# Feed-forwards in two parts of 14 and 8 gated tiles, with more chunks by seven block products

## The chip, the cores and the metric

The kernel runs on one core of a Trainium2 chip. The metric is the device time of one launch in microseconds. Data are fp32; the kernel splits each operand of a large product into a high and a low part and forms the product by three matmuls.

## The reference

Two blocks run one after the other over a sequence of 512 tokens of width 1024. The first has two layers of feed-forward, mixer, feed-forward and per-layer embedding (PLE); the second has two layers of mixer and feed-forward, scaled and shifted by a vector that a "modulation" product `silu(c) @ w_ada` gives. What the change touches is the six feed-forwards:

```python
def swiglu(h, w1, w3, w2):
    return (jax.nn.silu(h @ w1) * (h @ w3)) @ w2
def half_ffn(x, g, w1, w3, w2):                       # four times
    return x + FFN_RES * swiglu(rmsnorm(x, g), w1, w3, w2)
# second block, twice:
x = x + g2 * swiglu_2(h, w_gate_up[l], w_down[l])
```

with `h` of 512 x 1024, `w1` and `w3` of 1024 x 2816 and `w2` of 2816 x 1024. A PLE stage, `x + sigmoid(rmsnorm(x) @ ple_gate) * (p @ ple_proj)`, follows the second and the fourth feed-forward.

## The kernel before

Activations are held transposed: a tile is 128 features by 512 tokens. The 2816 gated features are 22 tiles. Weights come by DMA in chunks of 1024 x 256 (1 MB) into three buffers `raw`; ACT copies each 128 columns (a "run") to `wh` (high), DVE subtracts to get `wl` (low), and PE then does 8 k-tiles x 3 matmuls of 512 columns. There are three pairs `wh`/`wl` of 1024 elements, so DVE can split about two runs ahead of PE. A half-size buffer holds one part of a block product.

The four programs (PE, ACT, DVE and POOL, with SP issuing the weight DMAs) each walk the same list, which `rounds` yields for a feed-forward: for chunk pairs j = 0 to 10 the w1 chunk gives gate tiles 2j and 2j+1, the w3 chunk value tiles 2j and 2j+1. There is no scheduler; each engine works in order of this list, and DVE's and ACT's `step(g)` splits whatever weights have a free buffer when PE is about to do run g. After a plain w3 run `run_done` does, on DVE and ACT in turn: product with the gate (`gv`, tile `T`), ACT's high copy (`uh`), DVE's low part (`ul`). In the first four feed-forwards ("ffn") h is not yet divided by its root mean square; the tile `R` carries that factor and DVE multiplies every w1 and every w3 tile by it.

`WOVEN` names the chunks done by seven block products in place of eight (Strassen's scheme in Winograd's form, over halves of the 1024 features and of the 512 tokens). Before, these are both chunks of j = 2 to 6 in the last two feed-forwards ("ffn2"): 10 of 22, and none in the ffns. Such a chunk is 7 parts of 4 x 3 matmuls of 256 columns, 84 in all instead of 48 of 512 columns. `PARTS` = 1, 4, 6, 5 come first, then 7; parts 3 and 2 (`rest`) are put behind the next chunk's beginning. Part 6 goes on top of part 1 in the same bank, so PE first waits for ACT to copy part 1 out (`sq<-ps`, signal `curved p1`). DVE mixes quarters of the raw weights in place (`raw<-raw`, four per chunk), splits seven halves, and puts the tiles together (`joined`). The sums and differences of h that the parts need are made once per feed-forward by `differences`, beside the runs.

The output product walks four pairs of output tiles; for each pair three chunks of w2 with 8, 8 and 6 k-tiles, both tiles in each. DVE then adds the bank to x in one instruction.

The 48 modulation chunks ("ada") are not PE work: DVE reads each raw chunk with eight 256-wide multiply-adds, turns the sum in 32 x 32 squares and reduces it. Twelve are placed in each of the four ffns (`plan_ada`).

`inputs` (POOL) fetches `p` and `ple_proj` for a PLE stage into a region that the feed-forward uses for its tiles, so it waits until PE has finished a named run of w2 (L3629). PE's `enter` waits for both to land before it begins the PLE stage.

Of the kernel before, what the change touches and what calls it, by code (L numbers as in the profile page):

```python
# [169 lines left out]
WOVEN = {s: {(w, j) for j in range(2, 7) for w in ("w1", "w3")} if s[0] == "ffn2" else set() for s in FFNS}  # L170
PARTS = (1, 4, 6, 5)
SHARE = {1: (0, 0), 5: (0, 0), 3: (0, 0), 2: (1, 0), 4: (1, 1), 6: (1, 1), 7: (0, 1)}
# [4 lines left out]

def rounds(s):

    left = None  # L180
    for j in range(11):
        for w in ("w1", "w3"):
            if (w, j) in WOVEN[s]:
                for p in PARTS:
                    yield "part", w, j, p
            else:
                yield "run", w, 2 * j, 0
            if left:
                yield "part", *left, 3
                yield "part", *left, 2  # L190
                yield "joined", *left, 0
                left = None
            if (w, j) in WOVEN[s]:
                yield "part", w, j, 7
                yield "joined", w, j, 1
                left = w, j
            else:
                yield "post", w, 2 * j, 0
                yield "run", w, 2 * j + 1, 0
                yield "post", w, 2 * j + 1, 0  # L200


def build(nc, I, out):
    with ExitStack() as ctx:
# [123 lines left out]
        def plan_ffn(key, w1, w3, w2, with_ada):  # L328
            at = {}
            for what, w, i, p in rounds(key):  # L330
                j = i if what in ("part", "joined") else i // 2
                if what in ("part", "run") and (w, j) not in at:
                    at[w, j] = len(chunks)
                    chunks.append((8, 256, [(0, (w1 if w == "w1" else w3)[:, 256 * j:256 * j + 256])]))
                n = at[w, j] if (w, j) in at else None
                if what == "part":
                    G_of[(key, w, j, "part", p)] = n_mm[0]
                    part_of[n_mm[0]] = key, w, j, p
                    order.append(("mm", n_mm[0], n, p, 0, 0, 0))
                elif what == "run":  # L340
                    G_of[(key, w, i)] = n_mm[0]
                    order.append(("mm", n_mm[0], n, 128 * (i % 2), 128, 0, 8))
                else:
                    if what == "post" and w == "w3" and i % 2 and with_ada and j > 6:
                        plan_ada(1)
                    continue
                tail[n] = (lo_split, n_mm[0])
                n_mm[0] += 1
            for m in range(4):
                for k0, kt in ((0, 8), (8, 8), (16, 6)):  # L350
                    wide(key, ("w2", k0), w2, m * 256, 256, 2 * m, k0 * 128, kt)
                    if with_ada and (m < 2 or m == 2 and k0 < 16):
                        plan_ada(1)
# [160 lines left out]
        full = ar[:, 28:36, :]  # L514
        diff = ar[:, 6:14, :].rearrange("p a n -> p (a n)").rearrange(quads, c=4, k=4)
        diff_h = uh[:, 14:22, :].rearrange("p a n -> p (a n)").rearrange(quads, c=4, k=4)
        diff_l = ul[:, 14:22, :].rearrange("p a n -> p (a n)").rearrange(quads, c=4, k=4)
# [61 lines left out]
        def pe_program(e):  # L579
# [22 lines left out]
            def freed(s, name):  # L602
# [3 lines left out]
                if s[0] == "ffn2" and name[0] == "w3":  # L606
                    return (worked, (s, "gv", name[1]))
# [243 lines left out]

            def ffn(s, nxt):
                for what, w, i, p in rounds(s):
# [4 lines left out]
                if nxt is None:  # L858
                    chain = pe.beside(output())
                for m in range(4):  # L860
# [2947 lines left out]
```

## Time and profile before

| | us |
|---|---|
| time, median of 3 runs (range) | 3154.97 (3154.47 to 3155.27) |
| profiled execution's own time | 3154.14 |
| its span, first to last instruction | 3152.2 |
| PE busy | 3132.3 |
| DVE busy | 2013.7 |
| ACT busy | 1236.3 |

The profiled execution is 0.8 us below the median of the runs; 1.9 us of its time lie outside the span. PE's busy time counts a matmul from its start to its modelled end, so 99% says that PE hardly ever waits, not how dense its work is; the distance between two starts shows that.

### The profile page before, as it was taken

The numbers are of one execution on the slowest core, as the hardware profiler recorded it, in microseconds if no ns is written. First come the engines' busy times: TensorE is split into PE (matmuls) and PEld (weight loads), VectorE is DVE, ScalarE is ACT, GpSimd is POOL, SyncE is SP. The second block draws the span as 40 slices with busy tenths as digits, with TensorE's granted clock in tenths as the row PEclk, the third lists the DMA queues.
The fourth block names the chain that finished last, engine by engine and source line by source line (L and its number), as shares of the span: only waits on it lengthen the run. The fifth ranks groups of instructions, "written<-read, shape, count | busy, mean of one in ns | idle before, by whom it ended". The sixth has DMA issues, their size and how long they took to land.

```text
span 3152.2 us, 38120 instructions
## 1 busy us (share of the span) xinstructions
PE 3132.3 (99%) x15408; PEld 2618.7 (83%) x15408; DVE 2013.7 (64%) x2925; ACT 1236.3 (39%) x1812; POOL 157.8 (5%) x170
## 2 busy tenths in 40 slices
PE   9999999999999999999999999999999999999999
PEld 7888878888888888888888888887898888779887
DVE  5567567446856467557644685988893368889532
ACT  5322264322233222264332223565453235745321
POOL 2000000000000000000000000122000002300000
PEclk9999999999999999999999999999999999999999
DMA  5345322334542345432232463221233332022322
GB/s 151 97 131 190 124 84 94 94 96 145 190 137 81 94 133 181 140 94 81 86 102 94 147 192 117 82 70 41 78 111 104 100 87 84 28 80 95 120 87 74
DMA packets 334341, 339.92 MB, mean 108 GB/s; under 512 B 12502, under 2 KB 329208, under 8 KB 334168
## 3 DMA queue, kind: packets, MB, share of 16 engines
q1 hardware_dynamic: 332144, 333.80, 33.4%
q0 software_dynamic: 1792, 3.62, 0.4%
q8 instruction: 124, 2.03, 0.3%
q14 instruction: 49, 0.40, 0.0%
q10 hardware_dynamic: 232, 0.06, 0.0%
HBM read 335.36 MB, written 2.10 MB: 107 GB/s over the span
## 4 chain that ended last, share of the span: by engine, by line
PE 91%; DVE 5%; ACT 3%; issue 1%; DMA 0%; SPq 0%; DVEq 0%; ACTq 0%
PE ps L138 89%; PE ps L141 2%; ACT ar L95 1%; DVE wl L100 1%; DVE ar L100 1%; DVE ar L108 1%; ACT wh L95 1%; DVE ul L100 0%; ACT L95 0%; DVE T L108 0%; DVE hl L108 0%; ACT T L95 0%; ACT sp L95 0%; DMA ar<-in_x 0%; DVE T L100 0%
## 5 line engine op out<-in xcount | busy, mean ns | idle before, releaser
L138 PE MATMUL ps<-hh,wl 128*128 128x512 f32 (+1 forms) x2680 | 1026.4, 383 | 4.6 <-DVE wl L100 4.5
L100 DVE TENSOR_TENSOR wl<-raw,wh 128x1024 fp32r<-128x1024 f32 (+3 forms) x649 | 700.6, 1081 | 500.6 <-ACT wh L95 499.0
L138 PE MATMUL ps<-hh,wh 128*128 128x512 f32 (+1 forms) x2680 | 1019.2, 380 | 0.0
L138 PE MATMUL ps<-hl,wh 128*128 128x512 f32 (+1 forms) x2680 | 1019.0, 380 | 0.0
L95 ACT ACTIVATE wh<-raw 128x1024 fp32r<-128x1024 f32 (+3 forms) x649 | 602.5, 936 | 507.7 <-PE ps L138 462.0
L138 PEld LDWEIGHTS ps<-hh,wl 128*128 128x128 f32 x2680 | 504.8, 188 | 105.7 <-issue 11.0
L138 PEld LDWEIGHTS ps<-hh,wh 128*128 128x128 f32 x2680 | 505.0, 188 | 96.6
L138 PEld LDWEIGHTS ps<-hl,wh 128*128 128x128 f32 x2680 | 505.2, 189 | 93.2 <-issue 0.2
L138 PE MATMUL ps<-ul,wh 128*128 128x512 f32 (+1 forms) x1472 | 531.6, 366 | 0.0
L138 PE MATMUL ps<-uh,wl 128*128 128x512 f32 (+1 forms) x1376 | 503.7, 366 | 6.2 <-DVE wl L100 5.1
L138 PE MATMUL ps<-uh,wh 128*128 128x512 f32 (+1 forms) x1376 | 502.2, 365 | 0.0
L138 PEld LDWEIGHTS ps<-ul,wh 128*128 128x128 f32 x1472 | 278.5, 189 | 44.6
L138 PEld LDWEIGHTS ps<-uh,wl 128*128 128x128 f32 x1376 | 260.4, 189 | 47.6 <-ACT wh L95 6.7
L138 PEld LDWEIGHTS ps<-uh,wh 128*128 128x128 f32 x1376 | 260.3, 189 | 41.3
L95 ACT ACTIVATE uh<-T 128x512 fp32r<-128x512 f32 x132 | 83.4, 632 | 444.5 <-DVE T L100 444.1
L100 DVE TENSOR_TENSOR T<-ps,R 128x512 f32<-128x512 f32 x196 | 134.0, 689 | 176.3 <-PE ps L138 153.3
L95 ACT ACTIVATE T<-T 128x512 f32<-128x512 f32 (+1 forms) x112 | 68.6, 617 | 309.4 <-DVE T L100 309.1
L108 DVE SCALAR_TENSOR_TENSOR ada<-raw,small,ada 128x256 f32<-128x256 f32 x336 | 162.9, 485 | 12.0
L100 DVE TENSOR_TENSOR ul<-T,uh 128x512 fp32r<-128x512 f32 x132 | 91.4, 693 | 81.1 <-ACT uh L95 79.6
L100 POOL TENSOR_TENSOR small<-small 128x4 f32<-128x4 f32 (+1 forms) x23 | 38.1, 1655 | 1763.2 <-DVE small L123 996.6
L95 ACT ACTIVATE ar<-ar 128x512 f32<-128x512 f32 (+6 forms) x69 | 73.2, 1075 | 93.8 <-DVE ar L100 58.2
L95 ACT ACTIVATE hh<-x,VT 128x512 fp32r<-128x512 f32 x64 | 45.2, 720 | 161.3 <-DVE x L108 123.9
(257 smaller groups left out, 2791.3 us busy)
## 6 DMA issues: line engine op xcount, KB each, us to landing
raw<-in_ffn_w SPq DMA_DIRECT2D x119, 1024.0 KB, 5.3
raw<-in_w_ada SPq DMA_DIRECT2D x48, 1024.0 KB, 5.2
raw<-in_w_gate_up SPq DMA_DIRECT2D x44, 1024.0 KB, 5.1
raw<-in_m_w_in SPq DMA_DIRECT2D x26, 1024.0 KB, 5.4
raw<-in_w_down SPq DMA_DIRECT2D x16, 1024.0 KB, 5.1
raw<-in_ffn_w SPq DMA_DIRECT2D x16, 768.0 KB, 4.3
raw<-in_w_in SPq DMA_DIRECT2D x12, 1024.0 KB, 5.3
raw<-in_m_w_out SPq DMA_DIRECT2D x8, 1024.0 KB, 5.2
```

Source lines behind the costliest of these rows:

```text
L95: return self.issue(lambda e: e.activation(out, in_, func, **kw))
L100: return self.issue(lambda e: e.tensor_tensor(out, a, b, op))
L108: return self.issue(lambda e: e.scalar_tensor_tensor(out=out, in0=a, scalar=s, in1=b, op0=op0, op1=op1))
L138: return self.issue(lambda e: e.matmul(out, l, r, start=start, stop=stop, skip_group_check=True))
L141: return self.issue(lambda e: e.transpose(out, in_, ident))
```

## The change

`WOVEN` is a new set. In the ffns it holds the w3 chunk of j = 2, all w1 chunks of j = 3 to 10 and the w3 chunks of j = 4, 6 and 8: 12 of 22. In both ffn2s it holds w3 of j = 2, w1 of 3 to 10 and w3 of 3 to 9: the table comes to 16 of 22.

`rounds` now yields the output product too, and does a feed-forward in two parts: chunks j = 0 to 6 (14 gated tiles), then w2 chunks of 8 and 6 k-tiles for all eight output tiles; then j = 7 to 10 (8 tiles) and one w2 chunk of 8 k-tiles for each pair. Each output tile is therefore added to x twice (`added`). The second part's tiles reuse the slots of the first (`u_high`, `u_low`).

In the ffns `R` no longer multiplies the w3 tiles but the output banks, ahead of the addition to x, so an addition is two DVE instructions, twice per tile. A w3 tile's bank is read directly by the product with the gate. The plain chunk that follows a w1 chunk by block products has its two posts both behind its second run.

`differences` sums h in four pieces instead of two, and starts one step later except in the first stage. A modulation chunk is summed in two interleaved chains and one final addition. The modulation chunks of an ffn are now behind w3 runs 15 and 19, eight in the first output product and two in the second. The POOL wait in `inputs` names run ("w2", 14, 7), where it named ("w2", 0, 7).

```diff
-WOVEN = {s: {(w, j) for j in range(2, 7) for w in ("w1", "w3")} if s[0] == "ffn2" else set() for s in FFNS}
+WOVEN = {s: {("w3", 2), *((w, j) for j in range(3, 11) for w in ("w1", "w3") if w == "w1" or s[0] == "ffn2" or j % 2 == 0)} - {("w3", 10)} for s in FFNS}
...
+def parts_of(s):
+    if WOVEN[s]:
+        return (range(0, 7), ((0, 8), (8, 6))), (range(7, 11), ((14, 8),))
+    return (range(0, 11), ((0, 8), (8, 8), (16, 6))),
...
+    for js, ks in parts_of(s):
+        for j in js:
+            for w in ("w1", "w3"):
+                if (w, j) in WOVEN[s]:
+                    for p in PARTS:
+                        yield "part", w, j, p
+                    if left:
+                        yield from rest()
+                    yield "part", w, j, 7
+                    yield "joined", w, j, 1
+                    left = w, j
+                    continue
                 yield "run", w, 2 * j, 0
+                if left:
+                    yield from rest()
+                    left = None
+                    yield "run", w, 2 * j + 1, 0
+                    yield "post", w, 2 * j, 0
+                else:
+                    yield "post", w, 2 * j, 0
+                    yield "run", w, 2 * j + 1, 0
                 yield "post", w, 2 * j + 1, 0
+        for m in range(4):
+            for k in ks:
+                for a in range(2):
+                    yield "out", k, 2 * m + a, (k == ks[0]) + 2 * (k == ks[-1]) + 4 * (ks[-1][0] + ks[-1][1] == FT)
+                    if left:
+                        yield from rest()
+                        left = None
...
-                        dve.ts(adab[:, 0:256], src[:, 0, :], c_act[:, 0:1], MUL).then_inc(worked, ("ada", i, 0))
-                        for t in range(1, 8):
-                            dve.own()
+                        sums = adab[:, 0:256], adab[:, 256:512]
+                        for t in range(2):
+                            dve.ts(sums[t], src[:, t, :], c_act[:, t:t + 1], MUL).then_inc(worked, ("ada", i, t))
+                        for t in range(2, 8):
+                            dve.wait_ge(worked, ("ada", i, t - 2))
...
-                if s[0] == "ffn":
-                    dve.tt(T3[a][:, :], ps((s, "w3", t))[:, :], R[:, :], MUL).then_inc(left((s, "w3", t)), (s, "w3", t))
-                    dve.own()
-                    silu_done(s, t)
-                    dve.tt(T3[a][:, :], T3[a][:, :], T1[a][:, :], MUL).then_inc(worked, (s, "gv", t))
-                else:
-                    silu_done(s, t)
-                    dve.tt(T3[a][:, :], ps((s, "w3", t))[:, :], T1[a][:, :], MUL).then_inc(worked, (s, "gv", t))
+                silu_done(s, t)
+                dve.tt(T3[a][:, :], ps((s, "w3", t))[:, :], T1[a][:, :], MUL).then_inc(worked, (s, "gv", t))
...
-                if s[0] == "ffn":
+                if s[0] == "ffn" and w == "w1":
                     dve.own()
-                    dve.tt(to, to, R[:, :], MUL).then_inc(worked, (s, "gate" if w == "w1" else "value", t))
+                    dve.tt(to, to, R[:, :], MUL).then_inc(worked, (s, "gate", t))
...
             def differences(s):
-                for h in range(2):
-                    r = slice(4 * h, 4 * h + 4)
-                    for t in range(4 * h, 4 * h + 4):
+                if s != STAGES[0]:
+                    yield 1
+                for q in range(4):
+                    r = slice(2 * q, 2 * q + 2)
+                    for t in (2 * q, 2 * q + 1):
...
+            def added(s, nxt, t, p):
+                dve.wait_ge(used, end_run(s, t, p))
+                b = ps((s, "o", p & 4, t))
+                key = (x_new, (s, t)) if p & 4 else (worked, (s, "first", t))
+                if s[0] == "ffn":
+                    dve.tt(T1[t % 2][:, :], b[:, :], R[:, :], MUL).then_inc(worked, (s, "turned", p & 4, t))
+                    x_free(s, t)
+                    dve.own()
+                    dve.stt(x[:, t, :], T1[t % 2][:, :], 0.5, x[:, t, :], MUL, ADD).then_inc(*key)
+                    return
...
-                pool.wait_ge(used, G_of[(BEFORE[s], "w2", 0, 7)])
+                pool.wait_ge(used, G_of[(BEFORE[s], "w2", 14 if WOVEN[BEFORE[s]] else 0, 7)])
```

Two places in the order of DVE. The first is in the first ffn, at chunk pairs 3 and 4. Before, a plain w3 chunk and the first run of the next pair's w1 chunk stand as follows (`wl` is the low part of a run, `T_81`, `T_82` the value tiles, `ul` their low parts):

```order
L100 TENSOR_TENSOR T_81<-ps,R 128x512 [waits lo_part,weights_used]
L100 TENSOR_TENSOR T_81<-T_81,T_78 128x512 [waits curved,emptied3]
L100 TENSOR_TENSOR ul<-T_81,uh 128x512 [waits hi_part]
L100 TENSOR_TENSOR wl_65<-raw_58,wh_62 128x1024 [waits hi_split]
L100 TENSOR_TENSOR T_82<-ps,R 128x512 [waits lo_part,weights_used]
L100 TENSOR_TENSOR T_82<-T_82,T_79 128x512 [waits curved,emptied4]
L100 TENSOR_TENSOR ul<-T_82,uh 128x512 [waits hi_part]
L100 TENSOR_TENSOR wl_66<-raw_59,wh_63 128x1024 [waits hi_split]
```

Of the changed kernel, the end of w1 of pair 3 (joined and multiplied by `R`), the two posts of w3, and the first rows of the next w1 chunk by block products:

```order
L100 TENSOR_TENSOR T_78<-ps,sq_76 128x512 [waits weights_used]
L100 TENSOR_TENSOR T_78<-T_78,R 128x512 [waits emptied2]
L100 TENSOR_TENSOR wl_66<-raw_60,wh_63 128x512 [waits hi_split]
L100 TENSOR_TENSOR T_81<-ps,T_78 128x512 [waits curved,lo_part]
L100 TENSOR_TENSOR ul<-T_81,uh 128x512 [waits hi_part]
L100 TENSOR_TENSOR T_82<-ps,T_79 128x512 [waits weights_used]
L100 TENSOR_TENSOR ul<-T_82,uh 128x512 [waits hi_part]
L100 TENSOR_TENSOR wl_64<-raw_60,wh_61 128x512 [waits hi_split]
L100 TENSOR_TENSOR raw_60<-raw_60 128x4x128 [waits lo_split]
L100 TENSOR_TENSOR wl_64<-raw_58,wh_61 128x512 [waits hi_split]
```

The two posts moved from one behind each run to both behind the second, and what follows them is the split of small parts. The second place is the ACT order at the same point of the changed kernel; `uh` are the high copies of both value tiles, `wh` the high copies of two parts, `sq_75` the copy of part 1 for which PE's part 6 waits:

```order
L95 ACTIVATE T_78<-T_78 128x512 [waits worked]
L95 ACTIVATE uh<-T_81 128x512 [waits worked]
L95 ACTIVATE uh<-T_82 128x512 [waits worked]
L95 ACTIVATE wh_61<-raw_60 128x512 [waits weights_used]
L95 ACTIVATE wh_61<-raw_58 128x512 [waits raw_in0]
L95 ACTIVATE sq_75<-ps 128x256 [waits weights_used]
```

Before, ACT has only run splits, silus and `uh` copies there:

```order
L95 ACTIVATE wh_61<-raw_58 128x1024 [waits weights_used,raw_in0]
L95 ACTIVATE uh<-T_81 128x512 [waits worked]
L95 ACTIVATE wh_62<-raw_58 128x1024 [waits weights_used]
L95 ACTIVATE uh<-T_82 128x512 [waits worked]
L95 ACTIVATE wh_63<-raw_59 128x1024 [waits weights_used,raw_in1]
```

The copy `sq_75` is new there, and it stands behind both `uh` copies.

## Rows read from the trace of the kernel before

**Rows 1.** Page: engine, busy us (share) xinstructions; chain, shares by engine.

```profile
PE 3132.3 (99%) x15408; PEld 2618.7 (83%) x15408; DVE 2013.7 (64%) x2925; ACT 1236.3 (39%) x1812; POOL 157.8 (5%) x170
...
PE 91%; DVE 5%; ACT 3%; issue 1%; DMA 0%; SPq 0%; DVEq 0%; ACTq 0%
```

**Rows 2.** Waits of PE: waiter <- releaser: total us, times, longest us.

```profile
PE ps L138 <- DVE wl L100: 9.6, 7, 3.1
...
PE ps L138 <- ACT sq L95: 1.1, 1, 1.1
```

**Rows 3.** Windows: stretch, length, busy us (x) of PE, PEld, DVE, ACT, POOL, PEclk.

```profile
600.00:760.00 160.00, 160.00 (x708) 132.53 (x707) 85.86 (x110) 47.46 (x60) 0.00 (x0) 1.00 0.36 112
2270.00:2350.00 80.00, 80.00 (x669) 80.00 (x668) 74.20 (x117) 48.28 (x95) 0.00 (x0) 1.00 0.33 106
```

**Rows 4.** Timeline of PE, two starts: start us, us, engine, line, operation, tiles.

```profile
2274.71 0.28 PE L138 MATMUL ps<-hh,wl 128*128 128x256 f32 x1
...
2345.27 0.28 PE L138 MATMUL ps<-hh,wl 128*128 128x256 f32 x1
```

**Rows 5.** Timeline of PE, first block products of the fifth feed-forward.

```profile
2263.06 0.53 PE L138 MATMUL ps<-uh,wl 128*128 128x256 f32 x1 [3.13 <-DVE wl L100]
2263.39 0.42 PE L138 MATMUL ps<-ul,wh 128*128 128x256 f32 x1
2263.60 0.41 PE L138 MATMUL ps<-uh,wh 128*128 128x256 f32 x1
```

**Rows 6.** Timeline of DVE, entry of the fifth feed-forward.

```profile
2231.92 4.49 DVE L100 TENSOR_TENSOR ar<-hh,hl 128x2048 f32<-128x2048 f32 x2
...
2257.07 0.69 DVE L100 TENSOR_TENSOR T<-ps,T 128x512 f32<-128x512 f32 x1
...
2260.26 0.68 DVE L100 TENSOR_TENSOR T<-ps,T 128x512 f32<-128x512 f32 x1
```

**Rows 7.** Timeline of ACT, the same entry.

```profile
2260.98 0.63 ACT L95 ACTIVATE uh<-T 128x512 fp32r<-128x512 f32 x1 [1.52 <-DVE T L100]
2261.51 1.13 ACT L95 ACTIVATE wh<-raw 128x512 fp32r<-128x512 f32 x2
2262.55 0.36 ACT L95 ACTIVATE sq<-ps 128x256 f32<-128x256 f32 x1
```

**Rows 8.** Windows of DVE alone, three pairs of block-product chunks: sum and mean us.

```profile
sum 60.48, DVE 55.87; mean DVE 18.62
```

**Rows 9.** Timeline of DVE, inside block products.

```profile
2300.11 0.68 DVE L100 TENSOR_TENSOR T<-ps,acc 128x512 f32<-128x512 f32 x1
2300.83 0.69 DVE L100 TENSOR_TENSOR T<-T,T 128x512 f32<-128x512 f32 x1
2301.44 0.68 DVE L100 TENSOR_TENSOR wl<-raw,wh 128x512 fp32r<-128x512 f32 x1
```

**Rows 10.** Timeline of DVE, second feed-forward, one modulation chunk.

```profile
806.50 0.35 DVE L104 TENSOR_SCALAR ada<-raw,small 128x256 f32<-128x256 f32 x1
...
810.41 0.95 DVE L100 TENSOR_TENSOR wl<-raw,wh 128x768 fp32r<-128x768 f32 x1
811.39 0.45 DVE L126 STREAM_TRANSPOSE ada<-ada 128x256 f32<-128x256 f32 x1
811.87 0.42 DVE L123 TENSOR_REDUCE adaq<-ada 128x8 f32<-128x256 f32 x1
```

**Rows 11.** Timeline of POOL, DMAs for the first per-layer embedding stage.

```profile
896.96 0.80 POOL L77 DMA_DIRECT2D ar<-in_p  x1 [327.99 <-PE ps L138]
897.76 0.72 POOL L77 DMA_DIRECT2D ar<-in_ple_proj  x1
```

**Rows 12.** DMA issues: tiles, queue xcount, KB each, us to landing.

```profile
ar<-in_ple_proj POOLq DMA_DIRECT2D x2, 1024.0 KB, 6.2
```

**Rows 13.** Timeline of PE, end of run ("w2", 0, 7), first PLE instruction.

```profile
896.23 0.39 PE L138 MATMUL ps<-uh,wl 128*128 128x512 f32 x1
...
915.28 1.03 PE L141 MATMUL ps<-ident,ar 128*128 128x128 f32 x8
```

More of the change, by code:

```diff
@@ L331, in plan_ffn @@
                 j = i if what in ("part", "joined") else i // 2
[L332 to L353, printed above, removed]
+                if what in ("part", "run", "out"):
+                    if (w, j) not in at:
+                        at[w, j] = len(chunks)
+                        kt, move = 8, (w1 if w == "w1" else w3)[:, 256 * j:256 * j + 256] if what != "out" else None
+                        if what == "out":
+                            kt, move = w[1], w2[128 * w[0]:128 * (w[0] + w[1]), 256 * j:256 * j + 256]
+                        chunks.append((kt, 256, [(0, move)]))
+                    n = at[w, j]
+                    tail[n] = (lo_split, n_mm[0])
+                    if what == "part":
+                        G_of[(key, w, j, "part", p)] = n_mm[0]
+                        part_of[n_mm[0]] = key, w, j, p
+                        order.append(("mm", n_mm[0], n, p, 0, 0, 0))
+                    else:
+                        G_of[(key, "w2", w[0], i) if what == "out" else (key, w, i)] = n_mm[0]
+                        order.append(("mm", n_mm[0], n, 128 * (i % 2), 128, 0, chunks[n][0]))
+                    n_mm[0] += 1
@@ L355, in build @@
+                if with_ada and (what, w, i) in ADA_AFTER[bool(WOVEN[key])]:
+                    plan_ada(1)
         for st in STAGES:
@@ L1648, in differences @@
             def differences(s):
-                yield 1
-                yield 1
+                for _ in range(3 if s == STAGES[0] else 4):
+                    yield 1
                 for some in ((0, 2), (1, 3)):
@@ L1675, in ffn @@
                     act.beside(differences(s))
-                later = []
+                chain, later = None, []
                 for what, w, i, p in rounds(s):
@@ L2641, in ffn @@
                     dve.beside(differences(s))
-                later = []
+                chain, later = None, []
                 for what, w, i, p in rounds(s):
```

169 lines of the change are left out of this document (90 added, 79 removed).

## The prediction

> **What bounds the kernel now.** I read the page first: PE is busy for 99% of the span and 91% of the chain of waits is PE [rows 1]. So only two things move the time: how much PE time the work takes, and what PE waits for. The list of PE's waits comes next: DVE's weight splits (`wl`) cost 9.6 us in 7 waits and ACT's copy `sq` 1.1 us [rows 2]. The timeline puts all eight at the entries of the two last feed-forwards. They are caused by the block products' set-up; everywhere else PE runs without a break. The windows then give the pace of the two kinds of chunk. In 160 us of plain chunks 708 matmuls of 512 columns are counted, three of them overlapping the edges: 160/705.5 = 226.7 ns each, so a plain chunk of 48 takes 10.88 us. In 80 us of block products there are 669, less three: 120 ns [rows 3]. The timeline confirms it: from 2274.71 to 2345.27 are seven chunks, 10.08 us each, 84 x 120 ns [rows 4]. DVE is 54% busy in the plain stretch and 93% in the other [rows 3], so DVE is the engine to watch.
>
> **PE time.** Newly by block products are 12 chunks in each of four feed-forwards and 16 - 10 = 6 in each of the two last: 60. Each saves 10.88 - 10.08 = 0.80 us: -47.8 us. The output product keeps its 22 k-tiles per output tile, so splitting it costs PE nothing.
>
> The eighth product saved is an eighth of the columns (1.28 us at the same pace per column), yet only 0.80 us is to be had: a 256-column matmul costs 120 ns, more than half of 226.7. In the block products weight loads are busy for 80.00 of 80 us, in plain chunks for 132.5 of 160 [rows 3]. The Trainium skill, page "TensorE: Matmul & The Clock Gate", section "Back-to-back issue gap", gives N/2.4 + 2.5 ns between matmuls: 216 ns and 109 ns. By that a chunk would save 1.2 us and all 60 chunks 71 us, an estimate from the page. Its section on LDWEIGHTS speaks against the change instead: a load of 128 columns takes some 107 ns, so at 256 columns the loads come level with the matmuls. The trace agrees with the second and is above the first in both shapes; its 226.7 and 120 decide.
>
> **Entries of the two last feed-forwards.** What goes: of the 10.7 us of waits [rows 2] I count 10.3 as avoidable; the rest stands ahead of the runs in question. After the wait of 3.13 us the matmuls are 0.21 us apart and not 0.12 [rows 5]: the clock is at 1.2 GHz for about 17 matmuls, 1.6 us. I take the same for the other entry: 3.3. Together 13.6. Why they should go: `differences` put two sums of 4.49 us in one piece between two runs [rows 6]; these are now four pieces of a quarter, two per step, and start one run later in these stages. And the first block chunk is now w3 of pair 2, behind w1 runs, whose posts need nothing of DVE here; before it was w1 of pair 2, behind w3 posts. I let 1.1 us come back: -12.5.
>
> **PLE inputs.** POOL's two DMAs wait for a run of w2. Before, that run was done 19.0 us ahead of the feed-forward's end (896.23 to 915.28) [rows 13], POOL issued at 896.96 and 897.76 [rows 11], and landing takes 6.2 us [rows 12]: there at 904.0, 7.7 us after the run, 11 us early, and nothing was seen of it. Now ("w2", 14, 7) is the last run of the feed-forward. PE's first instruction of the PLE stage waits for the same DMAs, so PE stands for 7.7 us in each of two stages. Nothing else is queued for PE that could fill it. A stop of 3.13 us was followed by the low clock [rows 5], so I add 1.7 each: 2 x 9.4 = +18.8. Without a dip it is 15.4. DVE and ACT catch up in the meantime, which gains nothing, since PE waits for neither there today.
>
> **Plain w3 chunk to w1 chunk by block products, in the ffns.** This is new: it happens from pair 3 to 4, 5 to 6, 7 to 8 and 9 to 10, four places in each of four ffns, 16 in all. PE's part 6 waits for ACT's copy of part 1, ACT is behind its `uh` copy of the last value tile, and that waits for DVE's product. The entry of the fifth feed-forward shows the same chain: DVE's product at 2260.26 [rows 6], `uh`, two weight copies and `sq` ending at 2262.91 [rows 7], PE on at 2263.06 [rows 5], 2.8 us after the product began. Let T be the start of the second w3 run. It ends at T + 5.44; parts 1 and 4 take 2.88, so part 6 wants its start at T + 8.3. The product can begin at T + 5.6 at the earliest, part 6 then starts at T + 8.4: 0.1 us lost, plus whatever DVE is late. How late: independent DVE instructions of 512 are 0.61 us apart, dependent ones 0.72 [rows 9]. From T - 2.1 DVE has, for the next chunk, three part splits, three mixes, the joined tile and `R` (the waits on ACT included to T + 3.4), one more split, then the first post, which itself waits for a silu (product, ACT's copy, low part: 2.0 us) and ends at T + 6.2. So 0.6 late and 0.7 lost at pairs 3 and 5. At pairs 7 and 9 a modulation chunk comes in. Its sum takes 3.9 us before [rows 10] and about 3.2 in two chains (each of the old multiply-adds waited for the one before), which fits into the idle time ahead of T - 2.1; its turning and reduction (0.9 us, 811.39 to 812.3) [rows 10] falls inside the chain, so 1.6 lost. Per ffn 2 x 0.7 + 2 x 1.6 = 4.6, in four +18.4. Bounds: 0 if DVE is never late, 5.0 per place if each is as bad as 3.13 + 0.15 + 1.7 of clock [rows 5], 80 in all.
>
> **DVE's other load.** A pair of chunks by block products costs DVE 18.6 of 20.16 us [rows 8] and PE never waits there. In an ffn `R` adds two dependent instructions, 1.4 us: 20.1 of 20.16, and the next pair is only half so. That holds, narrowly; I give 0. The w3 tiles lose an `R` product (22 x 0.69) and the output gains one plus a second addition for each of eight tiles (about 24 instructions of 0.7): level, and in stretches where DVE keeps up. In the second output product DVE has, for each of eight tiles, a split of 1.2, two instructions of 0.7 for the addition and two for the norm, 33 us with waits, plus two modulation chunks of 4.1 us, in 43.5 us: up to 3 us late at the end, but the next stage's last tile is wanted only 9.5 us on. The start of block products in each ffn has `R` and silu ahead of the copy of part 1: 0.17 + 0.7 + 0.1 + 0.6 + 1.1 + 0.4 = 3.1 against 2.9, 0.2 us; with the small constants' chain in the first stage, whose steps now come every 1.4 us and not every 5.4, I put +3 in all.
>
> **Sum.** 3152.2 - 47.8 - 12.5 + 18.8 + 18.4 + 3.0 = 3132.1 span; 1.9 us lie around it: 3134.0. The profiled run before was 0.8 below the median, so 3134.9 is comparable with 3154.97. I say 3135, 0.6% faster.
>
> **Rivals.**
> - *The hand-overs are hidden.* DVE is early enough that neither posts nor modulation delay the copy, and no dip follows the PLE wait: 3152.2 - 47.8 - 13.6 + 15.4 + 1.9 + 0.8 = 3109. For it: 46% of idle DVE in plain stretches [rows 3]. Against it: the 0.1 us of room in the chain.
> - *DVE and ACT become the bound in the ffns.* Each of 16 places costs 5.0 us as the first one did [rows 5]: 3134.9 + 80 - 18.4 = 3196, slower. For it: the chain is the same one. Against it: there DVE was held up by 4.7 us of difference work in addition, here by none. It decides from 2.4 us per place on (47.8 + 12.5 - 18.8 - 3.0 = 38.5 us, by 16), where the whole gain is spent.
> - *The PLE wait does not bite,* if the DMA lands sooner or PE has work: 3135 - 19 = 3116. Against it: the code puts the wait on the last run and PE's wait first in the stage.
> - *The change does not do what it says.* Its words speak of 17 chunks in the last two; the table has 16. One more in each would save 1.6 us. Not a case of its own.
>
> **Chances.** Forecast 0.50 (3121 to 3148); hidden 0.20; slower rival with its weaker forms 0.20; PLE wait absent 0.10. A measurement of this kernel can tell 0.2%, 6.3 us, from no change. Of the slower rival about a third stays within that bound and the rest is above it; of the forecast's upper edge a little is within. So faster 0.79, same 0.08, slower 0.13. The range 3105 to 3162 holds the first, second and fourth case and the mild part of the third; the forecast's own is 3121 to 3148.
>
> **What would show it.** PE should have 60 x 36 more matmuls of the large products and about 84 x 120 ns per block chunk in the ffns too. The list of waits should have two waits for the DMA of `ple_proj`, 7 to 8 us each, followed by a lower clock. Waits for ACT `sq` should appear some 16 times in the ffns, 0.5 to 2 us each, and those for DVE `wl` at the entries of the last two feed-forwards should be gone. If PE's waits for DVE `wl` in the ffns sum to over 40 us, or if the block chunks there take more than 10.1 us each, the account is wrong.

## The result, and the profile after

The changed kernel takes 3186.68 us (median of 4 runs, 3185.42 to 3187.70) where the kernel before takes 3154.90: ratio 1.0101, 95% interval 1.0083 to 1.0118. It is slower by 31.8 us; 3135 was predicted, 0.6% faster, and 3162 was the upper end of the range. The profiled execution took 3187.7 us with a span of 3185.9, 33.7 more than before.

The page of the changed kernel, engine shares and the chain of waits:

```profile
PE 3101.5 (97%) x17568; PEld 2691.1 (84%) x17568; DVE 2410.4 (76%) x3709; ACT 1436.8 (45%) x2307; POOL 156.5 (5%) x170
...
PE 73%; DVE 17%; ACT 7%; issue 2%; DMA 1%; DVEq 0%; POOL 0%; SPq 0%; ACTq 0%; POOLq 0%
```

PE's share falls from 99% to 97% and its share of the chain from 91% to 73% [rows 1]. Its matmuls grow by 2160, which is 60 x 36, so all 60 new block chunks are there. The waits of PE, the largest groups, each waiter <- releaser: total us, times, longest us (before, the first two were DVE's `wl` with 9.6 and ACT's `sq` with 1.1 [rows 2]):

```profile
PE ps L138 <- ACT sq L95: 27.8, 24, 2.3
PE ps L138 <- DVE ul L100: 17.4, 4, 8.7
PE ps L141 <- DMA ar<-in_ple_proj: 15.6, 2, 7.9
PE ps L138 <- DVE wl L100: 12.9, 15, 1.7
PE ps L138 <- POOL small L129: 3.4, 1, 3.4
```

POOL's 3.4 was there before. I made an account from the start of every matmul: each is given the pace of its width, 226.7 or 120 ns [rows 3]. What lies over that by more than 0.3 us is a stop; what lies over it by less is the smaller excess. The latter is not all low clock: e2 has 21.1 us of it, at a granted clock of 1.000 over its span. What a kernel has above some 21 us is mostly low clock. The 7 to 8 us ahead of the first and behind the last matmul are in no row.

| us | before | after | e2 | e5 | e10 | e11 |
|---|---|---|---|---|---|---|
| matmuls of 512 and 256 columns at full pace | 2899.3 | 2851.2 | 2889.7 | 2851.2 | 2854.4 | 2855.2 |
| stops over 0.3 us | 13.3 | 82.9 | 4.1 | 42.9 | 29.3 | 21.1 |
| smaller excess | 25.8 | 35.3 | 21.1 | 30.9 | 28.2 | 26.4 |
| all other PE work | 207.0 | 208.7 | 206.7 | 206.2 | 207.0 | 206.3 |

(e2 to e11 are experiments below.) From before to after that is -48.1 + 69.6 + 9.5 + 1.7 = +32.7 of the 33.7; the other 1.0 lies ahead of the first and behind the last matmul. The first row is counts times pace, and the pace held: over 24 matmuls in a row the median distance is 120.0 and 226.7 ns in both kernels. PE time came out as predicted; the stops did not. By place they are, in the changed kernel: 35.1 at the hand-overs, 25.2 at the entries of the four ffns, 15.9 for the PLE inputs. About 10 us went at the entries of the two last feed-forwards (12.0 before, 1.9 after), and 3.5 came at other places, of which 2.5 are two waits for `wl` at the start of the stages behind the first and the third ffn.

**The entry of block products in an ffn.** DVE in the third ffn, the posts of four runs (`T`) and the low halves of the differences (`ul<-ar,uh`):

```profile
1043.84 0.68 DVE L100 TENSOR_TENSOR T<-ps,T 128x512 f32<-128x512 f32 x1
...
1049.71 0.68 DVE L100 TENSOR_TENSOR T<-ps,T 128x512 f32<-128x512 f32 x1
...
1055.03 2.35 DVE L100 TENSOR_TENSOR ul<-ar,uh 128x1024 fp32r<-128x1024 f32 x2
1057.30 0.68 DVE L100 TENSOR_TENSOR T<-ps,R 128x512 f32<-128x512 f32 x1
...
1060.42 2.35 DVE L100 TENSOR_TENSOR ul<-ar,uh 128x1024 fp32r<-128x1024 f32 x2
1062.69 0.69 DVE L100 TENSOR_TENSOR T<-ps,R 128x512 f32<-128x512 f32 x1
```

and PE, which needs these low halves for part 4:

```profile
1062.92 0.36 PE L138 MATMUL ps<-uh,wl 128*128 128x256 f32 x1 [3.06 <-DVE ul L100]
...
1065.49 0.36 PE L138 MATMUL ps<-uh,wl 128*128 128x256 f32 x1 [0.91 <-ACT sq L95]
...
1069.57 0.35 PE L138 MATMUL ps<-uh,wl 128*128 128x256 f32 x1 [0.97 <-ACT sq L95]
```

The posts are 5.87, 7.59 and 5.39 us apart, where PE's runs take 5.44. With 5.87 once more between 1037.97 and 1043.84, DVE has fallen 3.0 us behind over three runs, and PE waits 3.06 us. After it come, in the third and fourth ffn, two waits for `sq` of about 1 us, since DVE and ACT are still late; the first ffn has one of 1.9, the second one of 0.9. The waits for `ul` themselves are 3.23, 3.22 and 2.74 us (as excess over the pace) in the second to fourth ffn, and 8.87 in the first. In the first ffn DVE's posts start at 53.89, 59.76, 67.96 and 75.55: the step of 8.20 us holds the small constants that are made in this stage alone. That explains 2.3 us of the difference between 8.87 and the others; no run separates the rest.

**The hand-over from plain w3 to w1 by block products.** Pair 3 to 4 of the third ffn, PE:

```profile
1098.54 0.36 PE L138 MATMUL ps<-uh,wl 128*128 128x256 f32 x1 [0.54 <-DVE wl L100]
...
1102.69 0.36 PE L138 MATMUL ps<-uh,wl 128*128 128x256 f32 x1 [1.05 <-ACT sq L95]
```

and ACT there:

```profile
1096.45 0.63 ACT L95 ACTIVATE uh<-T 128x512 fp32r<-128x512 f32 x1 [1.36 <-DVE T L100]
1096.99 1.14 ACT L95 ACTIVATE wh<-raw 128x512 fp32r<-128x512 f32 x2
1098.03 0.36 ACT L95 ACTIVATE sq<-ps 128x256 f32<-128x256 f32 x1
...
1101.64 0.63 ACT L95 ACTIVATE wh<-raw 128x512 fp32r<-128x512 f32 x1 [2.73 <-DVE raw L100]
1102.18 0.37 ACT L95 ACTIVATE sq<-ps 128x256 f32<-128x256 f32 x1
```

On DVE the split of a part's weights stands behind both posts:

```profile
1097.11 0.69 DVE L100 TENSOR_TENSOR ul<-T,uh 128x512 fp32r<-128x512 f32 x1 [0.70 <-ACT uh L95]
1097.72 0.68 DVE L100 TENSOR_TENSOR wl<-raw,wh 128x512 fp32r<-128x512 f32 x1
```

The first wait, at part 6, is where it was predicted and of the predicted size (0.70 lost, 0.7 predicted). But the profile puts it down to DVE's `wl` and not to ACT's copy: the split ends at 1098.40, the copy at 1098.39. So two chains, both held up by the posts, end together here, and the prediction had one of them. Of the fifteen first waits eleven are put down to `wl` and four to `sq`. The second wait stands two parts on, at part 7: its bank also wants a copy by ACT (`sq` at 1102.18), and that stands behind a weight copy (1101.64) that waits 2.73 us for DVE's mix of quarters `raw`. The posts had pushed DVE's row of splits and mixes back, and by part 7 it has not caught up. The losses per ffn are 0.70 + 1.21, 0.70 + 1.21, 1.82 + 1.21 and 2.41: 9.26, against 4.6 in my sum. In the first ffn the hand-over from pair 3 to 4 costs nothing, for PE has other work just ahead of part 1 there, which gives DVE and ACT 1.9 us:

```profile
117.56 1.94 PE L138 MATMUL ps<-VT,ar 8*128 8x1 f32 x16
```

So fifteen hand-overs, and not sixteen, cost 35.1 us together.

**The PLE stage**, PE and POOL in the first of the two:

```profile
944.52 0.69 PE L141 MATMUL ps<-ident,ar 128*128 128x128 f32 x2 [7.66 <-DMA ar<-in_ple_proj]
```

```profile
937.42 0.80 POOL L77 DMA_DIRECT2D ar<-in_p  x1 [354.78 <-PE ps L138]
938.23 0.71 POOL L77 DMA_DIRECT2D ar<-in_ple_proj  x1
```

7.66 us of waiting, 7.82 above the pace, and 8.09 in the other: 7.7 was predicted. The granted clock in the first, in windows before and after the wait's end (it is the column ahead of the DMA share):

```profile
940.00:942.00 2.00, 0.00 (x0) 0.00 (x0) 1.12 (x3) 1.70 (x3) 0.00 (x0) 1.00 1.01 401
942.00:944.50 2.50, 0.00 (x0) 0.00 (x0) 1.75 (x2) 0.49 (x1) 0.00 (x0) 0.50 1.03 385
944.50:948.80 4.30, 4.28 (x14) 3.75 (x15) 3.64 (x6) 3.16 (x6) 0.00 (x0) 0.50 0.53 166
948.80:951.00 2.20, 2.20 (x11) 1.76 (x10) 0.06 (x1) 0.00 (x0) 0.00 (x0) 0.99 0.00 0
```

The clock falls to the lower of its two levels, 1.2 GHz, at 942.0, 5.1 us into the wait, and is back 4.3 us after PE resumed. Only half of these 4.3 is lost, 2.1 us; what passes at the low level while PE stands costs nothing. In the other stage the same is read: clock 0.50 from 1989.0, where PE resumes, to 1993.3. I had put 1.7.

### The profile page after: what moved, and what is told of

It is laid out like the page before. It is cut to its first block, busy times and chain, and to the rows that moved or that the text cites. A ratio compares the mean times of both kernels' runs of the same rounds, so it can differ in the third digit from the quotient of the medians.

```text
span 3185.9 us, 44190 instructions
## 1 busy us (share of the span) xinstructions
PE 3101.5 (97%) x17568; PEld 2691.1 (84%) x17568; DVE 2410.4 (76%) x3709; ACT 1436.8 (45%) x2307; POOL 156.5 (5%) x170
## 4 chain that ended last, share of the span: by engine, by line
PE 73%; DVE 17%; ACT 7%; issue 2%; DMA 1%; DVEq 0%; POOL 0%; SPq 0%; ACTq 0%; POOLq 0%
PE ps L138 71%; DVE wl L100 4%; DVE T L100 3%; DVE raw L100 2%; ACT wh L95 2%; PE ps L141 2%; ACT ar L95 1%; DVE ar L100 1%; DVE ul L100 1%; ACT uh L95 1%; DVE ada L108 1%; DVE ar L108 1%; ACT T L95 1%; DVE hl L108 1%; ACT L95 0%
## 5 line engine op out<-in xcount | busy, mean ns | idle before, releaser
L95 ACT ACTIVATE wh<-raw 128x512 fp32r<-128x512 f32 (+3 forms) x949 | 732.2, 785 | 787.5 <-PE ps L138 597.1
L100 DVE TENSOR_TENSOR wl<-raw,wh 128x512 fp32r<-128x512 f32 (+3 forms) x949 | 837.8, 888 | 296.3 <-ACT wh L95 292.5
L138 PE MATMUL ps<-hh,wh 128*128 128x512 f32 (+1 forms) x2440 | 849.2, 348 | 0.0
L138 PE MATMUL ps<-uh,wl 128*128 128x256 f32 (+1 forms) x2336 | 781.6, 335 | 55.9 <-ACT sq L95 27.8
L138 PE MATMUL ps<-ul,wh 128*128 128x256 f32 (+1 forms) x2432 | 806.1, 335 | 0.0
L138 PE MATMUL ps<-uh,wh 128*128 128x256 f32 (+1 forms) x2336 | 776.2, 332 | 0.0
L138 PEld LDWEIGHTS ps<-uh,wl 128*128 128x128 f32 x2336 | 447.1, 191 | 105.0 <-ACT wh L95 44.3
L138 PEld LDWEIGHTS ps<-ul,wh 128*128 128x128 f32 x2432 | 465.6, 191 | 44.1
L138 PEld LDWEIGHTS ps<-uh,wh 128*128 128x128 f32 x2336 | 447.2, 191 | 41.6
L100 DVE TENSOR_TENSOR raw<-raw 128x512 f32<-128x512 f32 x320 | 220.3, 688 | 11.4 <-DVE wl L100 0.5
```

The lines of the kernel that those rows point to most:

```text
L95: return self.issue(lambda e: e.activation(out, in_, func, **kw))
L100: return self.issue(lambda e: e.tensor_tensor(out, a, b, op))
L138: return self.issue(lambda e: e.matmul(out, l, r, start=start, stop=stop, skip_group_check=True))
```

## The experiments

Each change is against the changed kernel, unless it says otherwise. The kernel before took 3153.4 to 3153.9 us beside them. "e1" and so on number them.

| | what | us | ratio to before, 95% |
|---|---|---|---|
| e1 | PLE inputs early | 3170.06 | 1.0049, 1.0034 to 1.0064 |
| e2 | only the two last feed-forwards changed | 3131.70 | 0.9931, 0.9914 to 0.9947 |
| e3 | e2, and the ffns in two parts | 3132.96 | 0.9934, 0.9920 to 0.9949 |
| e4 | post held behind part 4 | 3184.33 | 1.0097, 1.0082 to 1.0112 |
| e5 | e1, and post held behind part 5 | 3141.31 | 0.9961, 0.9947 to 0.9976 |
| e6 | e1, and every w3 from pair 3 on by block products | 3229.98 | 1.0240, 1.0223 to 1.0257 |
| e7 | e1, without `R` on joined gate tiles (leaves part of the computation out) | 3150.45 | 0.9990, 0.9981 to 0.9999 |
| e8 | e1, and differences one run earlier | 3171.46 | 1.0055, 1.0040 to 1.0070 |
| e9 | e1, and the ffns' entry one chunk later | 3157.02 | 1.0008, 0.9998 to 1.0017 |
| e10 | e5 and e9 | 3127.36 | 0.9916, 0.9901 to 0.9931 |
| e11 | e10, and the first ffn one pair later | 3120.21 | 0.9895, 0.9879 to 0.9912 |
| e12 | e10 with late PLE inputs | 3145.45 | 0.9975, 0.9965 to 0.9985 |

### Which part of the change costs: e1, e2, e3

e1:

```diff
-  pool.wait_ge(used, G_of[(BEFORE[s], "w2", 14 if WOVEN[BEFORE[s]] else 0, 7)])
+  pool.wait_ge(used, G_of[(BEFORE[s], "w1", 10, "part", 2) if WOVEN[BEFORE[s]] else (BEFORE[s], "w2", 0, 7)])
```

> The changed kernel with POOL's two DMAs for a PLE stage waiting for the last part of the last w1 chunk (part 2 of pair 10), some 49 us before the feed-forward's end, and not for the last run of w2. Theory (the waits are real costs and add up): the two waits of 7.9 us for ple_proj go, and with them the low clock of 6.8 and 10.2 us behind them, worth half of that: 15.6 + 8.5 = 24 us, so 3163. Rival (DVE and ACT use the stop to catch up, so part of it comes back as other waits): 3170 to 3178. Rival (the wait is not what holds PE): 3187.

The wait is gone, and 16.6 us with it, less than the 24 expected, and in the range of the first rival (3170 to 3178). The 24 took the low clock of 6.8 and 10.2 us as standing behind the waits; only 4.3 us of each do, worth 2.1. And something is given back: in each of the two stages PE now waits 0.6 us for a `wl` for which it did not wait before, and in all the waits for `wl` grow from 12.9 to 14.1 us. The profiled execution of e1 was the fastest of its four, 3166.39; the others took 3170. e12 does the opposite in a kernel with few other waits.

e2, where `WOVEN` is empty for the ffns, and e3, where in addition `parts_of` gives the ffns the two parts:

```diff
-WOVEN = {s: {...} - {("w3", 10)} for s in FFNS}
+WOVEN = {s: {...} - {("w3", 10)} if s[0] == "ffn2" else set() for s in FFNS}
...
-    if WOVEN[s]:        # e3, in parts_of
+    if True:
```

> Only the two last feed-forwards are changed (two parts, 16 of 22 chunks); the first four have no block products and one part, as before, and the PLE wait is where it was. Theory (the loss lies in the four first feed-forwards and the PLE stages): 12 chunks x 0.80 us and the old entry waits of 13.6 us are gained, 3155 - 9.6 - 13 = 3132. Rival (splitting into two parts, with each output tile added twice, costs PE time wherever it is done): 3145 or more.

> As the one before, but the first four feed-forwards are done in two parts of 14 and 8 tiles too, still with no block product; R at the output, modulation chunks placed as in the changed kernel, PLE wait after the first third of the first output product, early enough. Theory: the split itself is free, 3132 as the one before, within 3 us. Rival (the second addition and R at the output, 12 us more of DVE per feed-forward beside the modulation chunks, delay PE): 3140 to 3150.

Both as expected. The 12 more block chunks and the new entries in the last two feed-forwards are worth 22 us, the two terms of the sum (9.6 and 12.5) together; in the list of waits of e2 hardly any for `wl` and `sq` are left:

```profile
PE ps L138 <- DVE wl L100: 1.1, 4, 0.3
PE ps L138 <- ACT sq L95: 0.8, 2, 0.4
```

The split into parts, with the second addition and the new places of the modulation chunks, costs some 1.3 us (`R` is at the output in both). From e3 to the changed kernel only the 48 block chunks of the ffns and the late PLE inputs are added. The chunks should gain 38.4 us, and 53.7 are lost: 92 us of stops and slower clock, of which the PLE inputs are 16.6 (e1).

### The hand-over: e4, e5, e7

The post of the second value tile is taken out of its place behind the plain w3 chunk and put among the parts of the next w1 chunk (the modulation chunks then follow the runs, not the posts):

```diff
+                        if p == 4:                     # e4; e5: p == 5
+                            while held:
+                                yield held.pop()
...
+                    if w == "w3" and j + 1 in js and ("w1", j + 1) in WOVEN[s]:
+                        held.append(("post", w, 2 * j + 1, 0))
+                        continue
```

> The changed kernel, where a plain w3 chunk is followed by a w1 chunk by block products the post of the second w3 tile is moved behind part 4 of that chunk, on DVE and ACT, so ACT copies part 1 before it waits for DVE's product. PLE wait as in the changed kernel. Theory (the hand-over chain product, high copy, copy of part 1 is what PE waits for, 9.3 us per feed-forward, and DVE has room otherwise): most of 37 us and 5 us of low clock go, 3150 to 3160. Rival (DVE itself is too late there, and the order of its work matters little): PE's waits for sq turn into waits for wl, 3178 to 3190.

A miss: 2.4 us gained, where 26 to 36 were expected; the time is in the rival's range, but the waits are again for `sq` and not for `wl`. ACT in the third ffn shows why:

```profile
1091.53 0.39 ACT L95 ACTIVATE sq<-ps 128x256 f32<-128x256 f32 x1 [0.28 <-PE ps L138]
...
1096.03 0.63 ACT L95 ACTIVATE uh<-T 128x512 fp32r<-128x512 f32 x1 [3.59 <-DVE T L100]
...
1097.08 0.36 ACT L95 ACTIVATE sq<-ps 128x256 f32<-128x256 f32 x1
```

The copy for part 6 is now in time (1091.53, PE does not wait there). But the held post reaches DVE behind its weight work, so ACT's `uh` waits 3.59 us (1096.03), and the copy for part 7 (1097.08) is queued behind it. Two waits of 0.70 and 1.21 have become one of 1.94. e5 moves the post one place on, behind that copy:

> With the early PLE wait (3170 with that alone), and the held post of the second w3 tile behind part 5 of the next chunk, one step of the order further than behind part 4, so that ACT's copies of part 1 and of parts 1+6 both stand ahead of it. Theory (the order of the hand-over decides: PE waits for a copy that stands behind the post): the 1.9 to 3 us per hand-over go, 3170 - 25 = 3145 to 3150. Rival (DVE's amount of work between two plain runs decides, and moving it only moves the wait, as behind part 4): 3167 to 3172, with waits on another part.

```profile
1069.50 0.63 ACT L95 ACTIVATE uh<-T 128x512 fp32r<-128x512 f32 x1 [0.83 <-DVE T L100]
...
1071.64 0.39 ACT L95 ACTIVATE sq<-ps 128x256 f32<-128x256 f32 x1 [0.28 <-PE ps L138]
...
1074.80 0.63 ACT L95 ACTIVATE wh<-raw 128x512 fp32r<-128x512 f32 x1 [2.26 <-DVE raw L100]
1075.34 0.36 ACT L95 ACTIVATE sq<-ps 128x256 f32<-128x256 f32 x1
```

Both copies, 1071.64 and 1075.34, are in time, and the hand-over from pair 3 to 4 costs nothing. Behind the entry of the third ffn four stops are left: 1.10 and 0.42 us at the hand-overs to pairs 8 and 10, and 0.73 and 0.71 us at w1 of pairs 5 and 9, where there was none. From e1, 28.8 us are gained (20 to 25 were expected) by the order alone, with as many instructions on DVE, ACT and PE: stops fall from 67.1 (e1) to 42.9 us. The order that changed is that of the posts and, at pairs 7 and 9, also that of the modulation chunks; no run tells the two apart there. At pairs 3 and 5, which have no modulation chunk, the 1.91 us of each hand-over go by the post alone.

e7, the lines that are left out:

```diff
-   dve.own()                                        # e7
-   dve.tt(to, to, R[:, :], MUL).then_inc(worked, (s, "gate", t))
```

> With the early PLE wait; the multiplication by R of gate tiles that come from block products is left out in the first four feed-forwards (64 dependent DVE instructions of 0.72 us, 46 us of DVE work), so the gates there are not normalised. It leaves part of the computation out. Rival theory (DVE's amount of work at the hand-over): each hand-over waits 0.7 to 1.4 us less, since DVE reaches the product of the last w3 tile earlier, 3170 - 16 x 1.4 = 3148 to 3160. First theory (position in the order): the post of the first w3 tile no longer waits for R, so also something, but no more than 0.7 each: 3159 to 3166.

e7 leaves the gate tiles of block chunks without the factor `R`. Two DVE instructions fewer per pair, in the old order, give 19.6 us, some 1.2 per hand-over; the theory of the order had allowed for 4 to 11, the rival for 10 to 22. The first wait goes behind pairs 3 and 5 and becomes 0.84 and 0.95 behind pairs 7 and 9, but the second, of 1.21, stays at all three places. So how much DVE has to do ahead of the posts counts too, beside where they stand.

### The rival, everything by block products: e6

```diff
-WOVEN = ... if w == "w1" or s[0] == "ffn2" or j % 2 == 0 ...
+WOVEN = ... {("w3", 2), *((w, j) for j in range(3, 11) for w in ("w1", "w3"))} ...
```

> With the early PLE wait; in the first four feed-forwards the w3 chunks of pairs 3, 5, 7 and 9 are done by block products too, 16 of 22 chunks as in the last two, so no plain w3 chunk stands between block products. The twelve modulation chunks stay as many, two of them now behind the joined tiles of w3 of pair 7. Theory (hand-overs from plain to block products are what costs): 9.3 us per feed-forward of waits go and 4 x 4 x 0.80 are gained, 3170 - 37 - 13 + something for modulation = 3125 to 3140. Rival (DVE is the bound: 20.1 of 20.16 us per pair by my count, with R, and modulation on top): DVE falls behind all the way, 3175 to 3200.

The waits of PE (the 17.4 us for `ul` are there as in e1):

```profile
PE ps L138 <- ACT sq L95: 70.3, 60, 3.7
PE ps L138 <- DVE wl L100: 18.9, 11, 5.3
```

The ffns have 16 block chunks of 22 here, and the two modulation chunks of pairs 7 and 9 both stand behind w3 of pair 7. This kernel has no plain w3 chunk between block products and hence no hand-over of the kind above, and is 60 us slower than e1, 30 beyond even the rival's range. With `R` on every pair DVE is busy for 55.8 of 60 us (690 to 750), and PE waits 0.4 to 1.1 us at every chunk from pair 4 to 6 and 3 to 4 us at four places behind the two modulation chunks. So DVE is the bound, and the plain w3 chunks let it catch up. How much of the 60 us comes from the modulation chunks standing together was not tried by itself.

### The entry: e8, e9, e10, e11

e8 starts `differences` one run earlier in the second to fourth ffn (on DVE as shown, and alike on ACT):

```diff
-                if s != STAGES[0]:
+                if s[0] == "ffn2":
                     yield 1
```

> With the early PLE wait; in feed-forwards 2 to 4 the sums and differences of h begin one run earlier (as they do in the first). Theory (part 4 of the first block-product chunk waits for the last low differences, 3.2, 3.2 and 2.7 us, because DVE makes them in the run just ahead): these three waits go, and with them one or two stretches of low clock, 3170 - 9 to 14 = 3156 to 3161. Rival (DVE is 4.6 us late from the posts and the mixes, whatever the place of the differences): the waits stay above 1.5 us each, 3166 to 3170.

The time is that of e1 within the scatter, nearest to the rival. The `ul` waits of these three are gone, and waits for `sq` of about 4 us stand in their place, here of 4.02:

```profile
1053.83 0.55 PE L138 MATMUL ps<-uh,wl 128*128 128x256 f32 x1 [4.02 <-ACT sq L95]
```

The lateness moved with the work: DVE has as much to do before the first block chunk, whatever the order. e9 gives it time instead, by leaving the w3 chunk of pair 2 plain:

```diff
-... {("w3", 2), *((w, j) for j in range(3, 11) ...)} ...
+... {*((w, j) for j in range(3, 11) ...)} ...                       # ffns only
```

> As e1 (PLE inputs fetched before the last w1 chunk), and in the four ffns the w3 chunk of pair 2 is plain again: block products begin with w1 of pair 3, two plain runs later (11 of 22 chunks). Theory (DVE comes to the entry 4.6 us late because splits, differences and posts of three runs exceed their 5.44 us each; two more plain runs leave it some 5 us of idle time to catch up): the four waits for `ul` at part 4 (17.4 us in sum) and the copies behind them (about 6 us) go; the chunk costs 4 x 0.80 = 3.2 us more; but the new entry is a hand-over from plain w3 to w1, worth 0.70 + 1.21 as at pair 3-4, in four places 7.6. So 3170 - 23.4 + 3.2 + 7.6 = 3157, less some 4 us of low clock: 3153 to 3158. Rival (the lateness is carried along, as when the differences started one run earlier): `ul` or `sq` waits of the same sum reappear at the new entry, 3170 + 3 = 3173 or more.

The time is as expected, 3157.02, but in part by luck. All four `ul` waits are gone: two plain runs, 10.9 us, are enough for DVE. The new hand-over from pair 2 to 3, for which 1.9 us were set down, costs nothing in the second to fourth ffn; the losses of 0.69 + 1.22 stay where they were, at pair 3 to 4. A likely reason, not tried by itself, is that the gate tiles of pair 2 come from plain runs, so DVE has no joined tile ahead of the posts. Against that, the first ffn gained little: stops of 0.95, 4.82 and 3.87 us (the second at the new entry, the third at pair 3 to 4) stand there in place of 8.87 and 2.41.

> As e5 (early PLE inputs, the second w3 post held until part 5 is set up), and block products begin in the ffns with w1 of pair 3 as in e9. Theory: the costs of entry and hand-over add up and go separately, so from e5 (3141.3) the `ul` waits of 17.4 us and about 6 us of copies behind them go, 3.2 us come back for the four plain chunks, the new hand-over costs up to 1 us in each of four ffns: 3141.3 - 23.4 + 3.2 + 3 = 3124, less some 4 us of low clock: 3119 to 3126, faster than the kernel before and than e2 (3131.7). Rival: with the lateness carried along 3141 or more; if entry waits go but hand-over waits come back because DVE has less slack, about 3135.

3127.36, 1.4 us above the upper end of what was expected of it, and 14 below e5. The two cures add up, and this is 0.84% faster than the kernel before. The largest share of what is left, 11.6 of 29.3 us of stops, is in the first feed-forward, where PE waits 4.66 us for `sq`, and ACT has this ahead of the copy:

```profile
87.13 1.28 ACT L95 ACT_TABLE_LOAD   x1
88.51 0.31 ACT L95 ACTIVATE small<-small 128x8 f32<-128x8 f32 x2
89.11 0.63 ACT L95 ACTIVATE uh<-T 128x512 fp32r<-128x512 f32 x1 [0.29 <-DVE T L100]
89.65 0.61 ACT L95 ACTIVATE wh<-raw 128x512 fp32r<-128x512 f32 x1
90.17 0.36 ACT L95 ACTIVATE sq<-ps 128x256 f32<-128x256 f32 x1
```

The table load of 1.28 us and `small` belong to constants that are made once, in the first stage. With them ACT loses 2.0 us between 87.13 and 89.11, less than half of the wait. e11 lets block products begin one pair later there, with w1 of pair 4:

```diff
-... for j in range(3, 11) ...
+... for j in range(4 if s == FFNS[0] else 3, 11) ...
```

> As e10, and in the first feed-forward alone block products begin with w1 of pair 4 (10 chunks there, 11 in the other three). Theory: of e10's 7.9 us lost at that entry (4.82 at 85.7 us, 1.87 and 1.21 two chunks on) 4.8 come from the first stage's small constants (two table loads of ACT of 1.28 us each and DVE's small sums stand between the copies that PE's part 6 waits for); with the entry at pair 4 those are done, so the 4.8 go and up to half of the other 3.1, while the plain chunk costs 0.8: 3127.4 - 4 to 5.5 = 3122 to 3123.5. Rival: the constants are also spread over the following posts and the new entry waits as long: 3128.

7.2 us gained where 4 to 5.5 were expected; stops fall by 8.2 and the smaller excess by 1.8 us, for 0.8 of PE time. The run moves the entry away from the constants and gives DVE two more plain runs at once, so what the table loads alone cost is not shown. At 3120.21 us, 1.05% faster than the kernel before and 2.1% faster than the changed one, it is the best version found. All stops at its hand-overs are 1.2 us or less.

### The price of the late PLE inputs: e12

The diff of e1, undone in e10.

> As e10, but the PLE inputs are again fetched only after the last w2 run. The wait itself is two times 7.8 us = 15.6 here as in the changed kernel. Theory A (waits and the low clock behind them add to whatever else the kernel loses): 3127.4 + 15.6 + 3.4 to 8 for low clock = 3146 to 3151. Theory B (part of the stop is given back, because DVE and ACT catch up during it and leave fewer waits behind it; undoing it in the changed kernel gained 16.6 only): 3127.4 + 15.6 = 3143 or less.

18.1 us. That lies between the two theories, at 3145.45 nearer to the first (from 3146) than to the second (to 3143). In the account stops grow by 14.8 us, since 15.8 come at the PLE inputs and two of 0.35 behind them, while two stops for `wl` of 0.8 each in the same stages go; smaller excess and other PE work grow by 3.2. The prediction's 18.8 was right in size.

## Why the prediction was wrong

- *PE time, -47.8*: right. -48.1 by the account, at paces that held; e2 came within 0.1 us of what its 12 chunks and its two entries should give, and e3 shows that the split is nearly free. (The 1.28 us that the text gives for the eighth product is not at the pace of 226.7 ns: an eighth of 10.88 is 1.36. Nothing rests on it.)
- *Entries of the two last feed-forwards, -12.5*: right. e2 gained 22.0 us, the two terms give 22.1; the waits for `wl`, which were to be gone there, are 0.3 us at most.
- *PLE inputs, +18.8*: right; 18.1 in e12 and 16.6 in e1, with a loss of 7.8 and 8.1 (7.7 predicted) and 2.1 us of clock behind it (1.7). My sentence that the catching up of DVE gains nothing was wrong by a little: without the stop PE waits 0.6 us for a `wl` in each of these stages.
- *Hand-overs, +18.4*: this step failed, by 17 us. The first waits had almost the predicted size (0.70, 0.70, 1.82, 2.41 against 0.7, 0.7, 1.6, 1.6). That the numbers fit so well is in part luck, since at eleven of fifteen places the profile names DVE's split, which the chain did not have. I followed the chain to the first copy that PE needs and stopped there. There is a second copy two parts on, and DVE's lateness was still there: 1.21 more at three of four places. 35.1 instead of 18.4, without the clock. e5 shows that the order of the posts decides, e7 that DVE's amount of work does too.
- *Start of block products in the ffns, +3.0*: this step failed most, by 22 us: 25.2 were measured. The step set ACT's and DVE's instructions of the last run against PE's parts and found 0.2 us. It took DVE to be on time when that run began. "DVE's other load" counted a pair of chunks in the steady state and the posts, but never the three runs ahead of the entry, in which the differences are made: 5.87 + 5.87 + 7.59 = 19.3 us against 16.3. e8 shows that the lateness is one of amount, e9 that two more plain runs remove it in the second to fourth ffn. In the first, where 8.87 + 1.86 us were lost, e9 leaves nearly as much, and e11, another pair later, gains 7 us; which part of that belongs to the small constants stays open.
- *DVE's other load, 0*: nearly right. Two waits for `wl` of 1.4 and 1.1 us come behind the output product of the first and third ffn, where e2 has 0.5 and 0.5.
- *Low clock*: apart from the two PLE stages my sum had none. The smaller excess has grown by 9.5 us and other PE work by 1.7, although the 3.3 at the two old entries are gone. Which of the short waits brings a dip and which doesn't stays open.

The sum with these in place: 3132.1 + (35.1 - 18.4) + (25.2 - 3.0) = 3171.0. The 14.9 us to 3185.9 are nearly all the 11.2 of smaller excess and other PE work and the 3.5 of stops at other places. Of the rivals, "DVE and ACT become the bound in the ffns" was the one that came true, in its weaker form: 35.1 + 25.2 us over its 16 places are 3.8 each, past its point of 2.4. Its argument against, that no difference work is added here, held for the hand-overs and was wrong for the entry.

## What to carry to other kernels

Where an engine prepares work for another, add up its work over all the steps since it was last surely ahead, not over the last step alone: lateness collects, and moving the same work earlier or later only moves the wait. Follow a late chain past the first instruction that it delays, on both engines that it runs through: here a second copy, 4 us on, cost 1.2 us more. The order of a queue is also a cure: putting one post (and, at half the places, a modulation chunk) elsewhere, with not an instruction less, was worth 29 us.

## What the runs showed of the hardware that I had not expected

- The granted clock can fall while PE shows no idle time. In the kernel before, PE is busy for the whole of the window below and its clock is 0.66; the last stop over 0.3 us was 160 us earlier. But busy is not dense: what stands just ahead of the dip, which starts at 170.7, are 1.94 us with sixteen matmuls of one column each. In the changed kernel sixteen like them (117.56, above) are followed by no dip.

```profile
168.13 1.94 PE L138 MATMUL ps<-VT,ar 8*128 8x1 f32 x16
...
170.00:175.00 5.00, 5.00 (x16) 3.98 (x16) 3.72 (x12) 1.56 (x2) 0.00 (x0) 0.66 0.36 125
```

- The dip does not begin at the wait's end: in the PLE stage it began inside the wait (above). Behind a wait of 2.25 us in the second ffn matmuls of 256 columns are still 0.12 us apart up to 873.71, and 0.21 from 873.88 on:

```profile
872.92 0.36 PE L138 MATMUL ps<-uh,wl 128*128 128x256 f32 x1 [2.25 <-ACT sq L95]
...
873.59 0.29 PE L138 MATMUL ps<-uh,wh 128*128 128x256 f32 x1
873.71 0.38 PE L138 MATMUL ps<-uh,wl 128*128 128x256 f32 x1
873.88 0.41 PE L138 MATMUL ps<-ul,wh 128*128 128x256 f32 x1
```

- The mean clock of the span overstates the loss: 0.993 of 3185.9 us is some 45 us at the lower level and would cost 22 us of work. But about a third of it lies where PE stands: 2.5 and 5.9 us in the two PLE waits (to 944.5, and 1983.1 to 1989.0), and some 6 us in the wait at the first entry, where the mean clock is 0.65 from 72.3 to 81.1. The smaller excess is 14.2 us above that of e2.
